# Low-rank products placed between blocks of four modulation-weight slots, and one group of loads issued in another order

## The reference

```
mod = (silu(c) @ ada_w + ada_b).reshape(B, 6, D)       # per layer
h   = rmsnorm(x) * (1 + mod[:, 1]) + mod[:, 0]
xx  = shifted(h) - h
w   = tanh((h + xx*mu[1]) @ w1)       # 2048 x 96
a   =      (h + xx*mu[4]) @ a1        # 2048 x 96
g   = sigmoid((h + xx*mu[5]) @ g1)    # 2048 x 256
r, k, v = (h + xx*mu[i]) @ (wr, wk, wv)                # then the recurrence, @ wo
x   = x + mod[:, 2] * out
x   = x + mod[:, 5] * relu(norm2(x) @ w1)**2 @ w2      # hidden width 8192
```

## Time and profile before

| | |
|---|---|
| median of 3 runs | 3504.15 us (3503.82 to 3504.71) |
| the profiled execution | 3496.72 us, its span 3495.2 us |
| PE busy | 3316.4 us (95% of the span) |
| DVE, ACT, POOL busy | 2036.0, 1419.5, 108.1 us |
| mean granted TensorE clock | 0.980 of full speed |
| DMA | 666.63 MB, mean 191 GB/s |

### The profile page before, as it was taken

The page is one execution under the profiler, slowest core; times in us unless marked ns, Lnnn a source line. Parts: engine busy times, 40 slices in busy tenths (PEclk is TensorE's granted clock), DMA queues, the critical chain, the costliest instruction groups (busy, mean ns, idle before and its releaser), DMA issues.

```text
span 3495.2 us, 80783 instructions
## 1 busy us (share of the span) xinstructions
PE 3316.4 (95%) x31616; PEld 3091.3 (88%) x31616; DVE 2036.0 (58%) x3433; ACT 1419.5 (41%) x2278; POOL 108.1 (3%) x206
## 2 busy tenths in 40 slices
PE   6899989889898999999999889999999999999998
PEld 2699978778787999999999888899898999999998
DVE  3434446666545877877777765545545545445454
ACT  2333325555435433324333374433435434343342
POOL 0000000000000000000000100000000000000000
PEclk8999999999999999999999989999999999999999
DMA  9777740000376888888888732243234444545442
GB/s 365 267 280 282 288 147 16 15 17 16 111 297 221 302 308 297 304 302 289 298 301 304 253 129 85 97 151 113 86 133 141 172 162 156 175 152 173 162 155 107
DMA packets 181905, 666.63 MB, mean 191 GB/s; under 512 B 21254, under 2 KB 21424, under 8 KB 181072
## 3 DMA queue, kind: packets, MB, share of 16 engines
q1 hardware_dynamic: 160416, 587.26, 46.4%
q0 software_dynamic: 21296, 76.60, 6.6%
HBM read 659.68 MB, written 4.09 MB: 190 GB/s over the span
## 4 chain that ended last, share of the span: by engine, by line
PE 88%; DVE 4%; DMA 3%; issue 2%; ACT 2%; SPq 0%; DVEq 0%; ACTq 0%; POOLq 0%
PE ps L1790 23%; PE ps L1792 22%; PE ps L1791 22%; PE ps L1905 6%; PE ps L1754 2%; DMA sb_raw<-stream 2%; PE ps L1912 2%; PE ps L1765 1%; PE ps L2189 1%; PE ps L2191 1%; PE ps L2190 1%; DVE sb_wlo L1063 1%; PE ps L1877 1%; ACT sb_whi L639 1%; DMA sb_strip<-strips 1%
## 5 line engine op out<-in xcount | busy, mean ns | idle before, releaser
L1063 DVE TENSOR_TENSOR sb_wlo<-sb_raw,sb_whi 128x1024 fp32r<-128x1024 f32 x778 | 942.5, 1223 | 627.5 <-ACT sb_whi L639 618.7
L639 ACT ACTIVATE sb_whi<-sb_raw 128x1024 fp32r<-128x1024 f32 x778 | 811.8, 1057 | 1120.3 <-PE ps L1792 984.4
L1790 PE MATMUL ps<-sb_ah,sb_whi 128*128 128x288 f32 x3728 | 1117.0, 300 | 44.4 <-DVE sb_al L1214 21.2
L1791 PE MATMUL ps<-sb_ah,sb_wlo 128*128 128x288 f32 x3728 | 1105.8, 297 | 0.0
L1792 PE MATMUL ps<-sb_al,sb_whi 128*128 128x288 f32 x3728 | 1102.3, 296 | 0.0
L1790 PEld LDWEIGHTS ps<-sb_ah,sb_whi 128*128 128x128 f32 x3728 | 704.6, 189 | 72.4 <-issue 56.5
L1792 PEld LDWEIGHTS ps<-sb_al,sb_whi 128*128 128x128 f32 x3728 | 707.4, 190 | 0.0
L1791 PEld LDWEIGHTS ps<-sb_ah,sb_wlo 128*128 128x128 f32 x3728 | 705.6, 189 | 0.1
L1790 PE MATMUL ps<-sb_bh,sb_whi 128*128 128x288 f32 x2048 | 608.4, 297 | 2.4 <-DVE sb_x L1141 2.3
L1791 PE MATMUL ps<-sb_bh,sb_wlo 128*128 128x288 f32 x2048 | 604.7, 295 | 0.0
L1792 PE MATMUL ps<-sb_bl,sb_whi 128*128 128x288 f32 x2048 | 602.7, 294 | 0.0
(11 more groups left out here) (293 smaller groups left out, 3518.4 us busy)
## 6 DMA issues: line engine op xcount, KB each, us to landing
sb_raw<-stream SPq DMA_DIRECT2D x1102, 512.0 KB, 4.8
sb_strip<-strips POOLq DMA_DIRECT2D x124, 512.0 KB, 5.7
sb_x<-xT SPq DMA_DIRECT2D x1, 2304.0 KB, 15.7
sb_x<-xT POOLq DMA_DIRECT2D x1, 2304.0 KB, 10.0
yT<-sb_x SPq DMA_DIRECT2D x4, 576.0 KB, 2.8
sb_lwa<-lw POOLq DMA_DIRECT2D x16, 130.0 KB, 2.8
sb_lwg<-lw POOLq DMA_DIRECT2D x16, 130.0 KB, 2.4
sb_l1g<-l1g SPq DMA_DIRECT2D x2, 1024.0 KB, 20.0
```

The source lines that it names most:

```text
L639: nc.scalar.activation(whi[:, q % SPL, :], raw[:, n, :], ACT.Copy).then_inc(hi_ready, 1)
L1063: nc.vector.tensor_tensor(wlo[:, q % SPL, :], raw[:, n, :], whi[:, q % SPL, :], ALU.subtract).then_inc(lo_ready, 1)
L1790: mm(out, wh, xh, start=start, stop=False)
L1791: mm(out, wl, xh, start=False, stop=False)
```

## The change

It does two things. On SP, `behind_half` is cut into three functions, and for g = 1 alone they are called in another order: first the four product slots, then the four vectors slots, then the four product slots of group 1. For g of 2 and more the order stays. On TensorE, `vectors_group` of groups 2 to 7 is cut into two halves of four slots; the low-rank products of a quarter's block 0 stand between the halves of the even group, those of block 1 behind its second half and ahead of its `ada_finish`, and those of blocks 2 and 3 between the halves of the odd group. The order on VectorE and ScalarE, the products and the loads themselves are the same.

```
             def behind_half(g):
                 for i in range(BURST):
-                    sp.wait_ge(lo_ready, 2 * BURST * g + (BURST * (HALVED_AT // RAW - 2 - VECTORS) - 2 * BURST + i + 1))
-                    fetch(g * 12 + (HALVED_AT - 16 + i), BURST + i)
-                    sp.wait_ge(ada_used, BURST * g + (ADA_FULL - 2 * BURST + i + 1))
-                    fetch(g * 12 + (HALVED_AT - 12 + i), i)
+                    second_half(g, i)
+                    burst_slot(g, i)
+                first_half(g)
...
-            with sp.Fori(1, HALF_GROUPS + 2) as g:
+            for i in range(BURST):
+                second_half(1, i)
+            for i in range(BURST):
+                burst_slot(1, i)
+            first_half(1)
+            with sp.Fori(2, HALF_GROUPS + 2) as g:
                 behind_half(g)
...
+            def half_group(o, h):
+                for p in range(BURST * h, BURST * h + BURST):
+                    ada_slot(s, o, p)
+
-            def low_rank(quarter):
+            def low_rank(quarter, blocks=range(4)):
                 pe.wait_ge(lora1_in, 64)
-                for b in range(4 * quarter, 4 * quarter + 4):
+                for b in [4 * quarter + z for z in blocks]:
...
             vectors_group(1)
             for i in range(3):
-                vectors_group(2 * i + 2)
-                low_rank(i)
-                vectors_group(2 * i + 3)
+                half_group(2 * i + 2, 0)
+                low_rank(i, (0,))
+                half_group(2 * i + 2, 1)
+                low_rank(i, (1,))
+                ada_finish(2 * i + 2)
+                half_group(2 * i + 3, 0)
+                low_rank(i, (2, 3))
+                half_group(2 * i + 3, 1)
+                ada_finish(2 * i + 3)
             low_rank(3)
```

More of the change, by code:

```diff
@@ L509, in behind_half, with second_half, burst_slot, first_half @@
                 for i in range(BURST):
-                    sp.wait_ge(lo_ready, 2 * BURST * g + (BURST * (HALVED_AT // RAW - 2 - VECTORS) - 2 * BURST + i + 1))
-                    fetch(g * 12 + (HALVED_AT - 16 + i), BURST + i)
-                    sp.wait_ge(ada_used, BURST * g + (ADA_FULL - 2 * BURST + i + 1))
-                    fetch(g * 12 + (HALVED_AT - 12 + i), i)
+                    second_half(g, i)
+                    burst_slot(g, i)
+                first_half(g)
+            def second_half(g, i):
+                sp.wait_ge(lo_ready, 2 * BURST * g + (BURST * (HALVED_AT // RAW - 2 - VECTORS) - 2 * BURST + i + 1))
+                fetch(g * 12 + (HALVED_AT - 16 + i), BURST + i)
+            def burst_slot(g, i):
+                sp.wait_ge(ada_used, BURST * g + (ADA_FULL - 2 * BURST + i + 1))
+                fetch(g * 12 + (HALVED_AT - 12 + i), i)
+            def first_half(g):
                 for i in range(BURST):
```

## The result

The changed kernel takes 3471.39 us (median of 4 runs, 3467.03 to 3476.03) against 3503.99 us (4 runs, 3499.90 to 3504.71): a ratio of 0.9911, interval 0.9895 to 0.9927. That is 32.6 us less where 26.7 us were forecast. The direction and both places are as forecast; the time lies 2.6 us under the low end of the range.

A forecast was written before the change was run, and what follows sets the result against it. The prediction took TensorE, 95% busy, to lose time to a stalled load ring in the beginning and a late product slot in the first feed-forward group: 17 + 9.7 = 26.7 us, 3504.15 to 3477.5 us, range 3474 to 3488.

The forecast's parts named there:

- The transfers set the pace, 1.28 us a slot: Beginning, groups 3 to 7: 40 slots at 410 GB/s, so group 7's last slot lands at 103.9 us.
- The queue never runs dry: Beginning: with low-rank work in pieces, at most five of eight places fill, leaving three loads in flight, 3.8 us.
- The end: Beginning: group 7 ends on TensorE at 105.0 or 106.7 us against 122.67, a gain taken as 17 us.
- The rest moves as a whole: From group 7 to stage r the same chain moves earlier, at cost 0; stage r starts near 121 us.
- Part two: First feed-forward group: product slot 5 loaded before the burst's wait removes TensorE's 8.24 us wait; gain 9.7 us.
- The rival of the clock: Beginning: TensorE at half clock for half the work becomes the bound; part one brings 3.5 to 9 us; chance 0.13.
- The shift reaches the end: After both places: later TensorE work waits on its own chain, so the whole 26.7 us should reach the end.
- the sum: Whole kernel: 17 + 9.7 = 26.7 us off the median 3504.15 gives 3477.5 us; profiled execution 3470.0.
- the two terms: Part one, the beginning, 17 us; part two, the first feed-forward group, 9.7 us.

The follow-up runs named there:

- unfilled executions: Profiled executions of the kernel before (3503.99 us) and the changed kernel (3471.39 us) without the 11 extra TensorE products that nobody reads.
- the filled kernels: Changed kernel and kernel before, each with 11 unread TensorE products in the 2.7 us wait of both attention halves: 3468.95 and 3497.64 us.

## Why the prediction was wrong

**The steps that held.** *The transfers set the pace, 1.28 us a slot:* 40 slots were issued and 408 GB/s moved over 52 us; the last slot of group 7 landed at 103.84 us for 103.9. The Trainium skill (DMA: Bandwidth & Descriptors, Where 436 GB/s comes from) has the 358 GB/s by which it would have been 111 us; the trace, with one core running, disagrees. (As an estimate from that figure the gain would have been 111.2 - 103.9 = 7.3 us smaller; the prediction wrote some 6.) *The queue never runs dry:* SP's longest wait is 4.0 us. *The end:* group 7 at 105.27 us for 105.0 to 106.7, 17.4 us for 17. *The rest moves as a whole:* stage r at 121.12 us for 121. *Part two:* from the burst, the transpose was forecast after 1118.1 - 1081.5 = 36.6 us and comes after 36.77; 9.5 us for 9.7. The rival of the clock fell plainly: after the first block TensorE was granted 1.00 until 110 us. *The shift reaches the end:* not contradicted. From the transpose to the end the unfilled executions take 2370.5 us before and 2371.8 changed on average, and from stage r to the first burst 940.6 and 942.5; both differences are smaller than the scatter.

**The step that failed** is in the sum: "The median of the runs is 7.4 above it, and what is removed is removed in both: 3504.15 - 26.7 = 3477.5 us", with a range that "adds 2 us for another program's layout" and nothing for the scatter of the executions. Both halves of that step were off.

First, the base. The 40 executions of before in this study have a mean of 3501.6 us and a standard deviation of 3.9, so three that agreed within 0.9 us (3503.82 to 3504.71) looked far surer than they were. Their median lay 2.6 us above that mean; the profiled execution, 3496.7 us, lay 4.9 us below it. The 7.4 us between them were no fixed difference that both kernels share: the execution that was read had its group at the short end (46.27 us) and none of the falls behind the later gaps. That is also why the forecast for its own time, 3470.0 us, missed the changed kernel's profiled 3476.03: two falls took 5.4 of the 6 us.

Second, what is removed is itself what scatters. Against 105.5 us, the old beginning costs 13.8 to 19.8 us more, 16.9 on average over six executions; against 36.9 us, the old group costs 9.4 to 11.2 more, 10.3 on average. The sum of the means, 27.2 us, hardly differs from the 26.7 of the prediction, so the two terms were sized well; but their spread, 8 us in all, was no part of the range. By all runs of the study the gain is 3501.6 - 3471.7 = 29.9 us (40 and 11 executions, standard error 1.3), between the filled kernels 28.5 (0.9). The 2.7 us between 27.2 and 29.9 are about two standard errors, and no profile shows a place for them. The unfilled executions with a profile, four of before and three of the changed kernel, show less and not more: 3499.3 - 3474.0 = 25.3 us by their means (standard error 1.7). Whether the 2.7 are chance or a small gain elsewhere stays open.

So of the 6.1 us between forecast and result, 2.6 are the base, 3.2 the gain (29.9 for 26.7, of which 2.7 without a place), and 0.3 the four runs of the changed kernel. With 3.9 us for one run the medians of three and of four carry some 2 us each, 2.8 together (an estimate); with twice that the low end would have been near 3469 instead of 3474.

That the granted clock depends on more than the program could have been read from the Trainium skill (TensorE: Matmul & The Clock Gate, Part 1, the HAM clock gate), which calls the number of products at the lower clock run-variable for the same kernel; the runs here agree, with 1.3 us in the first low-rank piece and 2.7 us behind one gap.

## What to carry to other kernels

A long piece of work that reads nothing from a ring of slots should be cut to what the loads in flight cover: here pieces of 2 to 4 us among slots of 1.28 us kept eight places turning, and moving the same work in one piece gave about a third of the gain or less, in the one execution there is. Before a load is put behind a wait in a queue, look who needs it before that wait can end; two product slots behind it cost 6.7 us. And a stretch that waits on a clock that comes and goes costs a different time in each run: take its length from several executions, and let the range hold the scatter of the runs, also where the first three agree.

## What was not expected of the hardware

- The same idle time of 2.68 us, on the same instruction, was followed by half clock in nine of the eleven unfilled executions at the first gap and in ten at the second, twice for a shorter time at the second and once at the first; in the others the clock stayed full. A fall costs up to 2.7 us. Eleven products that nobody reads took both falls away and 3 to 5 us of the mean.
- A queue that has run empty does not come back at its rate at once: behind the long pieces TensorE could read single slots only 1.75 to 2.7 us after the one before (in the kernel before and in the one with the piece moved), where the running queue lands one each 1.28 us. So an empty queue costs more than the time it stood still.
- With the new order the end of group 7 is within 0.5 us in every execution, where the old one had 6 us. The whole time is not steadier by it: the standard deviation of the runs is 3.9 us before and 3.8 us in the changed kernel.
